# A decoder block on one core: x and the first weights in 256 KB pieces, position loads moved, zero products ahead of the first transposes, x transposed inside the rows

## The chip, the core and the metric

The kernel runs on one core of a Trainium2 chip. The core has a matrix engine (TensorE, PE in the rows), a vector engine (VectorE, DVE), a scalar engine (ScalarE, ACT), GpSimd (POOL) and SyncE (SP), which here only issues transfers. Each engine works through its own list of instructions in order; semaphores make one wait for another. Transfers between the main memory and the on-chip memory run on 16 DMA engines beside them. The metric is the device time of the whole program in microseconds, and less is better.

## What is computed

One decoder block for 256 tokens of width 1024, all in float32: a norm, an input projection, a gated linear attention (GLA) and a softmax attention side by side, an output projection, and a SwiGLU feed-forward part. The change touches only the start, which is the norm and the projection:

```python
def reference(x, positions, norm1_gain, w_in, w_gate_up, b_gate, ...):
    h = rms_norm(x, norm1_gain[l])
    proj = h @ w_in[l]
    gq, gk, gv, gr, g_low, mq, mk, mv = parts      # 256, 256, 512, 512, 16, 512, 512, 512 columns
    gate_logit = (g_low @ w_gate_up[l] + b_gate[l]).astype(jnp.float32)
    log_a = jax.nn.log_sigmoid(gate_logit) / GLA_GATE_TAU
    o_gla = gla_chunked(gq, gk, gv, log_a)          # cumulative sums of log_a
    q_m, k_m = rotary(mq, positions), rotary(mk, positions)
    ...
    x = x + concatenate([o_gla, o_moba]) @ w_out[l]
    x = x + (silu(h2 @ w_ffn_gate[l]) * (h2 @ w_ffn_up[l])) @ w_ffn_down[l]
    return rms_norm(x, final_norm_gain)
```

## The kernel before

**Precision and tiling.** The tokens lie in two tiles of 128 (T = 2), the width in eight chunks of 128 (KC = 8). Every large product is made of three fast ones: an operand is split into a rounded high half and the rest as a low half, and `product` (line 430) issues high x high (L433), high x low weights (L434) and low x high (L435), each with 512 columns. ScalarE makes the high halves, VectorE the low ones.

**Weights.** They come in units of 1 MB (2048 columns of 128 partitions), first into one of three buffers `raw`, then split into one of six `w_hi` and `w_lo`. `split` on ScalarE (L782) and on VectorE (L997) does one unit; semaphores `hi_ready` and `lo_ready` count them. Units 0 and 1 are the eight rows (chunks of 128 input features) of the first 512 columns, that is of gq and gk; two units make one block of 512 columns, six blocks the projection. SyncE issues unit u once the unit three before it has left `raw` (`raw_free`, line 302).

**The start.** SyncE's list: x in two halves of tokens (512 KB each, L278), unit 0 in two halves (L311), the gate's low weights (16 columns of 1024 rows, L313), units 1 and 2, small vectors, and then the gated units. GpSimd issues the positions and rotary frequencies (L369, L370) before it builds the identity matrix (L371, L372), then masks. TensorE transposes the norm's gain (L449), does four transposes of the identity (`warm_up`, L455), then the 16 transposes of x into `aux` (L462), then eight more of the identity. The norm's scale factor per token is applied after the projection, so x can be multiplied at once: ScalarE takes each transposed chunk times the gain into `aT_hi` (`take_xT`, L805), VectorE the low half into `aT_lo` (L1001). Unit 0 is split row by row (`split_first`, L811 on ScalarE, L1013 on VectorE). TensorE's `first_unit` (line 469) waits for all four halves of a row (x and weights, high and low) and then issues its six matmuls.

**After unit 0.** `gate_low` (L495, L496) is a product with the gate's 16 columns, in 16 matmuls of 256 columns. Its weights `low_w` are rounded by ScalarE (L821) and their low half made by GpSimd (L407). VectorE copies the result, `lowT` (L1025), and `logits` (L529) multiply it with the gate's second matrix. VectorE adds the bias (L1034), ScalarE and VectorE make `log_a` (L831 to L833, L1059; the sine's angles, made from the positions, are reduced in between, L1040 to L1065), and `cumulate` (L538, L540), in the middle of unit 3, sums them. The norm's factor `rstd` is made from sums of squares (ScalarE, L788) by two small GpSimd steps for each token tile (L402, L403). These orders are all written out by hand; no scheduler changes them. The rest, attention and eleven feed-forward phases, is not touched but for semaphore counts.

## Time and profile before

| | us |
|---|---|
| median of 3 runs | 314.44 |
| lowest and highest run | 314.31, 314.89 |
| the profiled execution | 314.29 |
| its span in the profile | 312.3 |
| TensorE busy in it | 301.4 |

The rows below come from the one profiled execution. A line of a timeline gives the start and the length of one instruction (or of several alike, with their count behind an x), its engine, its line in the kernel, the operation, what it writes and reads, and in brackets for how long the engine was idle before it and what released it. PE is the matrix engine's products, PEld its loading of the stationary operand, which overlaps them. The ends of matmuls are modelled, so neighbours seem to overlap by 0.1 to 0.2 us: the distance between two starts is what one costs. Counts of matmuls of float32 operands can be multiples of those in the program.

### The profile page before, as it was taken

How to read it: one execution, taken by the hardware profiler on the slowest of the kernel's cores; microseconds unless marked ns; L12 is line 12 of the kernel's file. 1: busy time of each engine (PE TensorE's matmuls, PEld its weight loads, DVE VectorE, ACT ScalarE, POOL GpSimd, SP SyncE). 2: the span in 40 equal slices, each digit the busy share in tenths (PEclk: the TensorE clock that was granted, in tenths of full speed). 3: DMA queues.
4: the chain of work that ended last, by engine and by line, in shares of the span. 5: the costliest groups of instructions: out<-in, count | busy, mean ns of one | idle time of the engine just before them, and what ended most of it. 6: DMA issues, size and time to landing. Idle time of an engine off the chain costs nothing.

```text
span 312.3 us, 3865 instructions
## 1 busy us (share of the span) xinstructions
PE 301.4 (97%) x1424; PEld 251.2 (80%) x1424; DVE 178.9 (57%) x199; ACT 153.7 (49%) x185; POOL 21.9 (7%) x44
## 2 busy tenths in 40 slices
PE   5899999999999999999999999999999999999992
PEld 5787888888888888888888888888888888888881
DVE  0888979986686247645371809082635536280434
ACT  2978897568553437361533526070807152443124
POOL 7130100000202001500000000000000000000002
PEclk9999999999999999999999999999999999999998
DMA  7986386537744303928374564729090918330003
GB/s 224 367 277 244 118 295 206 192 134 270 253 148 139 134 0 82 309 81 283 123 242 163 184 220 137 266 72 331 18 376 9 326 77 274 129 134 0 0 2 135
DMA packets 36449, 54.45 MB, mean 174 GB/s; under 512 B 2834, under 2 KB 25540, under 8 KB 36436
## 3 DMA queue, kind: packets, MB, share of 16 engines
q1 hardware_dynamic: 36356, 54.24, 51.1%
q0 software_dynamic: 64, 0.03, 0.3%
q8 instruction: 8, 0.13, 0.2%
q14 instruction: 5, 0.04, 0.0%
q10 hardware_dynamic: 16, 0.00, 0.0%
HBM read 53.23 MB, written 1.05 MB: 174 GB/s over the span
## 4 chain that ended last, share of the span: by engine, by line
PE 94%; DMA 2%; DVE 1%; ACT 1%; issue 0%; SPq 0%; POOLq 0%; POOL 0%; DVEq 0%
PE acc L433 16%; PE acc L435 15%; PE acc L434 15%; PE aux L435 13%; PE aux L433 13%; PE aux L434 13%; PE aux L522 4%; DMA raw<-in_w_in 2%; PE aux L600 1%; DVE x_sb L1188 1%; PE aux L622 1%; PE aux L582 1%; PE aux L568 1%; DVE reuse_e L1246 0%; ACT reuse_e L974 0%
## 5 line engine op out<-in xcount | busy, mean ns | idle before, releaser
L997 DVE TENSOR_TENSOR w_lo<-raw,w_hi 128x2048 fp32r<-128x2048 f32 x48 | 107.9, 2287 | 15.2 <-ACT w_hi L782 15.2
L782 ACT CAST w_hi<-raw 128x2048 fp32r<-128x2048 f32 x48 | 89.7, 1912 | 6.5 <-PE acc L435 4.6
L433 PE MATMUL aux<-w_hi,aT_hi 128*128 128x512 f32 x176 | 69.7, 396 | 0.0
L435 PE MATMUL aux<-w_hi,aT_lo 128*128 128x512 f32 x176 | 68.8, 391 | 0.0
L434 PE MATMUL aux<-w_lo,aT_hi 128*128 128x512 f32 x176 | 68.5, 389 | 0.0
L433 PE MATMUL acc<-w_hi,aT_hi 128*128 128x512 f32 x136 | 54.9, 403 | 1.1 <-DVE w_lo L1013 1.1
L435 PE MATMUL acc<-w_hi,aT_lo 128*128 128x512 f32 x136 | 53.1, 391 | 0.0
L434 PE MATMUL acc<-w_lo,aT_hi 128*128 128x512 f32 x136 | 53.0, 390 | 0.0
L1220 DVE TENSOR_TENSOR pT_lo<-aux,pT_hi 128x512 fp32r<-128x512 f32 x10 | 6.9, 692 | 70.6 <-ACT pT_hi L943 70.6
L943 ACT CAST pT_hi<-aux 128x512 fp32r<-128x512 f32 x10 | 5.9, 587 | 76.5 <-PE aux L522 76.5
L435 PEld LDWEIGHTS aux<-w_hi,aT_lo 128*128 128x128 f32 x176 | 33.0, 188 | 7.1
L434 PEld LDWEIGHTS aux<-w_lo,aT_hi 128*128 128x128 f32 x176 | 33.1, 188 | 6.6
L433 PEld LDWEIGHTS aux<-w_hi,aT_hi 128*128 128x128 f32 x176 | 33.0, 188 | 6.5
L433 PE MATMUL acc<-w_hi,pT_hi 128*128 128x512 f32 x80 | 31.2, 390 | 0.0
L435 PE MATMUL acc<-w_hi,pT_lo 128*128 128x512 f32 x80 | 31.1, 389 | 0.0
L434 PE MATMUL acc<-w_lo,pT_hi 128*128 128x512 f32 x80 | 31.1, 389 | 0.0
L433 PEld LDWEIGHTS acc<-w_hi,aT_hi 128*128 128x128 f32 x136 | 25.6, 188 | 6.6 <-issue 1.6
L435 PEld LDWEIGHTS acc<-w_hi,aT_lo 128*128 128x128 f32 x136 | 25.5, 188 | 5.5
L434 PEld LDWEIGHTS acc<-w_lo,aT_hi 128*128 128x128 f32 x136 | 25.6, 188 | 4.9
L930 ACT ACTIVATE reuse_c<-aux,rstd 128x256 f32<-128x256 f32 x22 | 10.4, 473 | 26.3 <-PE aux L435 26.2
L434 PEld LDWEIGHTS acc<-w_lo,pT_hi 128*128 128x128 f32 x80 | 15.0, 188 | 3.1
L435 PEld LDWEIGHTS acc<-w_hi,pT_lo 128*128 128x128 f32 x80 | 15.0, 188 | 3.1
(170 smaller groups left out, 237.4 us busy)
## 6 DMA issues: line engine op xcount, KB each, us to landing
raw<-in_w_in SPq DMA_DIRECT2D x24, 512.0 KB, 4.9
raw<-in_w_ffn_gate SPq DMA_DIRECT2D x22, 512.0 KB, 4.4
raw<-in_w_ffn_up SPq DMA_DIRECT2D x22, 512.0 KB, 5.5
raw<-in_w_ffn_down SPq DMA_DIRECT2D x22, 512.0 KB, 5.8
raw<-in_w_out SPq DMA_DIRECT2D x8, 512.0 KB, 4.0
x_sb<-in_x SPq DMA_DIRECT2D x2, 512.0 KB, 3.8
out<-reuse_e SPq DMA_DIRECT2D x4, 256.0 KB, 2.4
reuse_a<-in_final_norm_gain SPq DMA_DIRECT2D x1, 512.0 KB, 4.7
```

What stands on the lines that cost most here:

```text
L433: nc.tensor.matmul(dst, left_hi[:, k, tok], right_hi, start=first, stop=False)
L434: nc.tensor.matmul(dst, left_hi[:, k, tok], right_lo, start=False, stop=False)
L435: return nc.tensor.matmul(dst, left_lo[:, k, tok], right_hi, start=False, stop=last)
L522: last = nc.tensor.transpose(aux[:, bank, n * P:(n + 1) * P], src, ident[:, :])
L568: last = nc.tensor.matmul(aux[:, bank, pair * SEQ:(pair + 1) * SEQ], kiT[:, pair, tok], qdT[:, pair, :, tok], start=True, stop=True)
L582: last = nc.tensor.matmul(aux[:, 2 + h // 2, (h % 2) * SEQ:(h % 2 + 1) * SEQ], mT[:, 0, h, P:SEQ], mT[:, 1, h, :], start=True, stop=True)
L600: last = nc.tensor.matmul(aux[:, bank, h * DV:(h + 1) * DV], probT[:, t + k, h, :], mv[:, k, h * DV:(h + 1) * DV], start=k == 0, stop=k == t)
L782: nc.scalar.copy(w_hi[:, slot % RING, :], raw[:, slot % RAW, :]).then_inc(hi_ready, 1)
L930: nc.scalar.activation(silu_g[:, t, :], aux[:, GATE_UP_BANKS[parity][t], 0:FF], ACT.Silu, scale=rstd[:, 1, t:t + 1]).then_inc(silu_ready, 1)
L943: nc.scalar.copy(dst, aux[:, 1, :].rearrange("p (k s) -> p k s", k=2)).then_inc(hiddenT_hi_ready, 1)
L997: nc.vector.tensor_tensor(w_lo[:, slot % RING, :], raw[:, slot % RAW, :], w_hi[:, slot % RING, :].bitcast(f32), ALU.subtract).then_inc(lo_ ...
L1220: nc.vector.tensor_tensor(lo, aux[:, 1, :].rearrange("p (k s) -> p k s", k=2), hi.bitcast(f32), ALU.subtract).then_inc(hiddenT_lo_ready, 1)
```

## The change

It leaves the computed values' definition as it is and rewrites the first eight rows of weights:

- x comes in four parts of 256 columns for both token tiles, and units 0 and 1 in eight rows of 256 KB, in the order: a part of x, two rows, a part of x, two rows. `EARLY = 2` says that units 0 and 1 are treated by rows; the counts of `hi_ready` and `lo_ready` now begin with unit 2.
- GpSimd issues the positions and the frequencies behind the low half of the gate's weights.
- TensorE begins with six products of a zeroed buffer (`warm`, 256 columns), then the gain's transpose, five more, the first part of x, two more. The zeroing is VectorE's first instruction.
- A row of weights (`first_row`) waits for each of its four halves apart, and rows 1, 3 and 5 hold the four transposes of the next part of x ahead of their last two matmuls.
- `gate_low` and `other_gains` stand behind row 6 and ahead of row 7, `logits` behind row 7.
- VectorE rounds row 0 of the weights itself; the other seven stay with ScalarE, each one ahead of or behind a part of x.

```diff
+EARLY = 2
+X_PARTS = 4
...
-    return u // RAW + (1 if u % RAW else 0)
+    return u // RAW + (1 if u % RAW >= EARLY else 0)
...
+        warm = w_lo[:, RING - 1, 0:SEQ]
...
-            for t in range(T):
-                sp.dma_start(x_sb[:, t, :], x[0, t * P:(t + 1) * P, :]).then_inc(x_loaded[t], 16)
+            def x_part(p):
+                cols = slice(p * 2 * P, (p + 1) * 2 * P)
+                sp.dma_start(x_sb[:, :, cols], x[0, :, cols].rearrange("(t p) n -> p t n", p=P)).then_inc(x_loaded[p], 16)
+
+            def first_part(n):
+                sp.dma_start(raw[:, n // 4, (n % 4) * 512:(n % 4 + 1) * 512],
+                             w_in[0, n * P:(n + 1) * P, BLOCKS[0]:BLOCKS[0] + 512]).then_inc(first_loaded[n], 16)
+
+            for p in range(X_PARTS):
+                x_part(p)
+                for n in (2 * p, 2 * p + 1):
+                    first_part(n)
...
-                if isinstance(u, int) and u == RAW:
-                    sp.wait_ge(first_lo_ready, 4)
+                if isinstance(u, int) and u < RAW + EARLY:
+                    sp.wait_ge(first_lo_ready, 4 * (u - RAW + 1))
                 else:
-                    sp.wait_ge(lo_ready, u - RAW)
-
-            buf = raw[:, 0, :].rearrange("p (k n) -> p k n", k=4)
-            for h in range(2):
-                sp.dma_start(buf[:, 2 * h:2 * h + 2, :], w_in[0, 2 * h * P:2 * (h + 1) * P, BLOCKS[0]:BLOCKS[0] + 512]
-                             .rearrange("(k p) n -> p k n", p=P)).then_inc(first_loaded[h], 16)
+                    sp.wait_ge(lo_ready, u - RAW - EARLY + 1)
+
             sp.dma_start(low_raw[:, :, :], w_in[0, :, LOW:LOW + RANK].rearrange("(k p) n -> p k n", p=P)).then_inc(low_loaded, 16)
-            for u in range(1, RAW):
+            for u in range(EARLY, RAW):
                 rows_unit(u, w_in[0], (u % 2) * 4 * P, 4, BLOCKS[u // 2], 512)
...
-            with nc.allow_non_contiguous_dma(reason="256 positions, one per partition and tile"):
-                pool.dma_start(pos_i[:, :], positions.rearrange("b (t p) -> p (b t)", p=P)).then_inc(pos_loaded, 16)
-            pool.dma_start(freq[:, :], inv_freq.to_broadcast([P, HALF])).then_inc(pos_loaded, 16)
             then(nc.gpsimd.memset(ident[:, :], 0.0))
             nc.gpsimd.affine_select(out=ident[:, :], in_=ident[:, :], compare_op=ALU.not_equal, fill=1.0, base=0,
                                     pattern=[[-1, P]], channel_multiplier=1).then_inc(ident_built, 1)
...
             pool.wait_ge(low_hi_ready, 1)
             nc.gpsimd.tensor_tensor(low_w[:, :, :, 1, :], low_raw[:, :, :].unsqueeze(2).to_broadcast(LOW_COPIES),
                                     low_w[:, :, :, 0, :].bitcast(f32), ALU.subtract).then_inc(low_lo_ready, 1)
+            with nc.allow_non_contiguous_dma(reason="256 positions, one per partition and tile"):
+                pool.dma_start(pos_i[:, :], positions.rearrange("b (t p) -> p (b t)", p=P)).then_inc(pos_loaded, 16)
+            pool.dma_start(freq[:, :], inv_freq.to_broadcast([P, HALF])).then_inc(pos_loaded, 16)
             for t in range(T):
                 wide_rstd(0, t)
...
+            def warm_up(n):
+
+                for _ in range(n):
+                    nc.tensor.matmul(acc[:, 2, 0:SEQ], warm[:, 0:P], warm, start=True, stop=True)
+
+            pe.wait_ge(warm_built, 1)
+            warm_up(6)
             pe.wait_ge(ident_built, 1)
             pe.wait_ge(norm1_loaded, 16)
             nc.tensor.transpose(acc[:, 3, NORM1_ROW:NORM1_ROW + KC], gain_rows[0:KC, :],
                                 ident[0:KC, 0:KC]).then_inc(gains_in_psum, 1)
...
-            def warm_up(n):
-
-                for _ in range(n):
-                    nc.tensor.transpose(acc[:, 2, 0:P], ident[:, :], ident[:, :])
-
-            warm_up(4)
-            for t in range(T):
-                pe.wait_ge(x_loaded[t], 16)
-                for bank in range(4):
-                    for k in (2 * bank, 2 * bank + 1):
-                        last = nc.tensor.transpose(aux[:, bank, (k % 2) * SEQ + t * P:(k % 2) * SEQ + (t + 1) * P],
+            warm_up(5)
+
+            def x_transposed(part):
+
+                pe.wait_ge(x_loaded[part], 16)
+                for k in (2 * part, 2 * part + 1):
+                    for t in range(T):
+                        last = nc.tensor.transpose(aux[:, part, (k % 2) * SEQ + t * P:(k % 2) * SEQ + (t + 1) * P],
                                                    x_sb[:, t, k * P:(k + 1) * P], ident[:, :])
-                    if t == T - 1:
-                        last.then_inc(xT_in_psum, 1)
-
-            warm_up(8)
-
-            def first_unit():
-
-                for k in range(4):
-                    pe.wait_ge(xT_hi_ready, k + 1)
-                    pe.wait_ge(xT_lo_ready, k + 1)
-                    pe.wait_ge(first_hi_ready, k + 1)
-                    pe.wait_ge(first_lo_ready, k + 1)
-                    for t in range(T):
-                        last = product(acc[:, t, :], k, t, *weights(0, 512, k), k == 0, False)
-                last.then_inc(unit_used, 1)
+                last.then_inc(xT_in_psum, 1)
+
+            def first_row(k, next_part=None):
+
+                right_hi, right_lo = weights(k // 4, 512, k % 4)
+                toks = [slice(t * P, (t + 1) * P) for t in range(T)]
+                pe.wait_ge(xT_hi_ready, k + 1)
+                pe.wait_ge(first_hi_ready, k) if k else pe.wait_ge(row0_hi_ready, 1)
+                for t in range(T):
+                    nc.tensor.matmul(acc[:, t, :], aT_hi[:, k, toks[t]], right_hi, start=k == 0, stop=False)
+                pe.wait_ge(first_lo_ready, k + 1)
+                for t in range(T):
+                    nc.tensor.matmul(acc[:, t, :], aT_hi[:, k, toks[t]], right_lo, start=False, stop=False)
+                if next_part is not None:
+                    x_transposed(next_part)
+                pe.wait_ge(xT_lo_ready, k + 1)
+                for t in range(T):
+                    last = nc.tensor.matmul(acc[:, t, :], aT_lo[:, k, toks[t]], right_hi, start=False, stop=k == KC - 1)
+                    if k == KC - 1 and t == 0:
+                        last.then_inc(tile0_in_psum, 1)
+                if k % 4 == 3:
+                    last.then_inc(unit_used, 1)
 
...
-            after = {0: [gate_low, other_gains], 1: [logits], 4: [gla_transposed], 6: [gla_scores],
-                     7: [moba_scores], 9: [moba_outputs]}
-            for u in range(IN_UNITS):
-                if u == 0:
-                    first_unit()
-                else:
-                    in_unit(u, midway.get(u, ()))
+            after = {4: [gla_transposed], 6: [gla_scores], 7: [moba_scores], 9: [moba_outputs]}
+            x_transposed(0)
+            warm_up(2)
+            for k in range(7):
+                first_row(k, next_part=k // 2 + 1 if k in (1, 3, 5) else None)
+            gate_low()
+            other_gains()
+            first_row(7)
+            logits()
+            for u in range(EARLY, IN_UNITS):
+                in_unit(u, midway.get(u, ()))
...
-            def split_first(half):
-                act.wait_ge(first_loaded[half], 16)
-                for k in (2 * half, 2 * half + 1):
-                    nc.scalar.copy(w_hi[:, 0, k * 512:(k + 1) * 512], raw[:, 0, k * 512:(k + 1) * 512]).then_inc(first_hi_ready, 1)
+            def split_first(n):
+                act.wait_ge(first_loaded[n], 16)
+                cols = slice((n % 4) * 512, (n % 4 + 1) * 512)
+                nc.scalar.copy(w_hi[:, n // 4, cols], raw[:, n // 4, cols]).then_inc(first_hi_ready, 1)
 
 
             act.wait_ge(gains_ready, 1)
             take_xT((0, 1))
-            split_first(0)
-            take_xT((2, 3))
-            split_first(1)
-            take_xT((4, 5, 6, 7))
+            for p in range(1, X_PARTS):
+                split_first(2 * p - 1)
+                split_first(2 * p)
+                take_xT((2 * p, 2 * p + 1))
+            split_first(7)
             act.wait_ge(low_loaded, 16)
             nc.scalar.copy(low_w[:, :, :, 0, :], low_raw[:, :, :].unsqueeze(2).to_broadcast(LOW_COPIES)).then_inc(low_hi_ready, 1)
-            split(1)
+            split(2)
             for t in range(T):
-                act.wait_ge(x_loaded[t], 16)
                 sum_squares(0, t)
-            split(2)
             split(3)
             take_block(0, gqk)
...
-            def split_first(k):
-                dve.wait_ge(first_hi_ready, k + 1)
-                cols = slice(k * 512, (k + 1) * 512)
-                nc.vector.tensor_tensor(w_lo[:, 0, cols], raw[:, 0, cols], w_hi[:, 0, cols].bitcast(f32),
+            def split_first(n):
+                slot, cols = n // 4, slice((n % 4) * 512, (n % 4 + 1) * 512)
+                if n:
+                    dve.wait_ge(first_hi_ready, n)
+                else:
+                    dve.wait_ge(first_loaded[0], 16)
+                    nc.vector.tensor_copy(w_hi[:, 0, cols], raw[:, 0, cols]).then_inc(row0_hi_ready, 1)
+                    dve.wait_ge(row0_hi_ready, 1)
+                nc.vector.tensor_tensor(w_lo[:, slot, cols], raw[:, slot, cols], w_hi[:, slot, cols].bitcast(f32),
                                         ALU.subtract).then_inc(first_lo_ready, 1)
 
+            nc.vector.memset(warm.bitcast(f32), 0.0).then_inc(warm_built, 1)
             dve.wait_ge(gains_in_psum, 1)
             nc.vector.tensor_copy(gains[:, 0:KC], acc[:, 3, 0:KC]).then_inc(gains_ready, 1)
             dve.wait_ge(gains_ready, 1)
-            for k in range(4):
-                take_xT((k,))
-                split_first(k)
-            take_xT((4, 5, 6, 7))
-            split(1)
+            split_first(0)
+            take_xT((0, 1))
+            for p in range(1, X_PARTS):
+                split_first(2 * p - 1)
+                split_first(2 * p)
+                take_xT((2 * p, 2 * p + 1))
+            split_first(7)
```

TensorE around the gate's low product, before. `acc` and `aux` are accumulators, `ident` the identity; L433 to L435 are unit 0's last row and unit 1's first, L495 and L496 the low product.

```order
L433 MATMUL acc<-w_hi,aT_hi 128x512
L434 MATMUL acc<-w_lo,aT_hi 128x512
L435 MATMUL acc<-w_hi,aT_lo 128x512
L495 MATMUL acc<-aT_hi,w_hi 128x256 [waits xT_hi_ready,xT_lo_ready,low_lo_ready,low_hi_ready]
L496 MATMUL acc<-aT_lo,w_hi 128x256
...
L483 MATMUL acc<-ident,reuse_d 128x10 [waits rows_loaded,gains_ready]
L433 MATMUL acc<-w_hi,aT_hi 128x512 [waits lo_ready,hi_ready]
L434 MATMUL acc<-w_lo,aT_hi 128x512
L435 MATMUL acc<-w_hi,aT_lo 128x512
```

After, from the transposes inside row 5 on (L488, L491 and L496 are a row's three kinds, L477 the transposes, L517 and L518 the low product):

```order
L477 MATMUL aux<-ident,x_sb 128x128 [waits x_loaded_3]
L477 MATMUL aux<-ident,x_sb 128x128 x3
L496 MATMUL acc<-w_hi,aT_lo 128x512 [waits xT_lo_ready]
...
L488 MATMUL acc<-w_hi,aT_hi 128x512 [waits first_hi_ready,xT_hi_ready]
...
L491 MATMUL acc<-w_lo,aT_hi 128x512 [waits first_lo_ready]
...
L496 MATMUL acc<-w_hi,aT_lo 128x512 [waits xT_lo_ready]
...
L517 MATMUL acc<-aT_hi,w_hi 128x256 [waits xT_hi_ready,xT_lo_ready,low_lo_ready,low_hi_ready]
L518 MATMUL acc<-aT_lo,w_hi 128x256
...
L505 MATMUL acc<-ident,reuse_d 128x10 [waits rows_loaded,gains_ready]
L488 MATMUL acc<-w_hi,aT_hi 128x512 [waits first_hi_ready,xT_hi_ready]
...
L491 MATMUL acc<-w_lo,aT_hi 128x512 [waits first_lo_ready]
```

The low product stood behind four rows and ahead of the other four; it now stands behind seven, and each row's matmuls are grouped by kind with a wait for each.

ScalarE from the second half of unit 0 on, before (L805 takes transposed x, L811 rounds a row, L821 the gate's low weights, L782 a whole unit, L788 the squares):

```order
L811 CAST w_hi<-raw 128x512 [waits first_loaded_1]
L811 CAST w_hi<-raw 128x512
L805 ACTIVATE aT_hi<-aux,gains 128x256 [waits xT_in_psum] x4
L821 CAST w_hi<-low_raw 128x32x16 [waits low_loaded]
L782 CAST w_hi<-raw 128x2048 [waits raw_loaded_1]
L788 ACTIVATE reuse_f,ss<-x_sb 128x1024 [waits x_loaded_0]
L788 ACTIVATE reuse_f,ss<-x_sb 128x1024 [waits x_loaded_1]
L782 CAST w_hi<-raw 128x2048 [waits raw_loaded_2]
```

After, from the rounding of row 6 on (L831, L837, L848, L808 and L814 are the same five):

```order
L837 CAST w_hi<-raw 128x512 [waits first_loaded_6]
L831 ACTIVATE aT_hi<-aux,gains 128x256 [waits xT_in_psum] x2
L837 CAST w_hi<-raw 128x512 [waits first_loaded_7]
L848 CAST w_hi<-low_raw 128x32x16 [waits low_loaded]
L808 CAST w_hi<-raw 128x2048 [waits raw_loaded_2]
L814 ACTIVATE reuse_f,ss<-x_sb 128x1024 x2
L808 CAST w_hi<-raw 128x2048 [waits raw_loaded_0]
```

The low weights' rounding stands behind the last two chunks of x in both, but these now follow the transposes that TensorE does inside row 5.

VectorE, before, from the last chunks of x to the logits' sum (L1001 low half of x, L997 low half of a unit, L1025 the copy of the low product):

```order
L1001 SCALAR_TENSOR_TENSOR aT_lo<-aux,gains,aT_hi 128x256 [waits xT_hi_ready]
L1013 TENSOR_TENSOR w_lo<-raw,w_hi 128x512 [waits first_hi_ready]
L1001 SCALAR_TENSOR_TENSOR aT_lo<-aux,gains,aT_hi 128x256 [waits xT_hi_ready] x4
L997 TENSOR_TENSOR w_lo<-raw,w_hi 128x2048 [waits hi_ready]
L1025 COPY lowT<-acc 32x256 [waits low_in_psum]
L1027 COPY gains<-acc 128x10 [waits gains_in_psum]
L997 TENSOR_TENSOR w_lo<-raw,w_hi 128x2048 [waits hi_ready] x2
```

After (L1043 is the low half of one row, L1022 of a unit, L1058 the copy):

```order
L1043 TENSOR_TENSOR w_lo<-raw,w_hi 128x512 [waits first_hi_ready] x2
L1026 SCALAR_TENSOR_TENSOR aT_lo<-aux,gains,aT_hi 128x256 [waits xT_hi_ready] x2
L1043 TENSOR_TENSOR w_lo<-raw,w_hi 128x512 [waits first_hi_ready]
L1058 COPY lowT<-acc 32x256 [waits low_in_psum]
L1060 COPY gains<-acc 128x10 [waits gains_in_psum]
L1022 TENSOR_TENSOR w_lo<-raw,w_hi 128x2048 [waits hi_ready] x2
```

The split of a whole unit that stood ahead of the copy is gone (it was unit 1's); unit 2's and unit 3's stay behind it.

## Rows read from the trace of the kernel before

**Rows 1.** Page: busy time of each engine; the chain's shares by engine.
```profile
PE 301.4 (97%) x1424; PEld 251.2 (80%) x1424; DVE 178.9 (57%) x199; ACT 153.7 (49%) x185; POOL 21.9 (7%) x44
...
PE 94%; DMA 2%; DVE 1%; ACT 1%; issue 0%; SPq 0%; POOLq 0%; POOL 0%; DVEq 0%
```

**Rows 2.** Chain of waits to 25 us: start, length, what.
```profile
1.71 6.44 DMA raw<-in_w_in
...
9.66 0.47 PE acc L433
```

**Rows 3.** Timeline, TensorE and VectorE: start, length, engine, line, operation.
```profile
15.19 0.28 PE L495 MATMUL acc<-aT_hi,w_hi 128*128 128x256 f32 x1
...
16.98 0.28 PE L496 MATMUL acc<-aT_lo,w_hi 128*128 128x256 f32 x1
...
17.30 0.41 DVE L1025 COPY lowT<-acc 32x256 f32<-32x256 f32 x1
...
24.15 0.50 PE L433 MATMUL acc<-w_hi,aT_hi 128*128 128x512 f32 x1
...
32.45 0.81 PE L538 MATMUL aux<-reuse_b,tri_mid 128*128 128x256 f32 x3
```

**Rows 4.** Tile x_sb, first 25 us: issues on SyncE; from issue to landing.
```profile
L278 SPq DMA_DIRECT2D x_sb<-in_x x2: 382/402/421, 0.8 to 1.2; - x2
...
DMA to landing us min/median/max: 3.4/3.8/4.3
```

**Rows 5.** One window (last: clock, DMA share, GB/s); issues: KB, us to landing.
```profile
6.00:7.00 1.00, 1.00 (x7) 1.00 (x6) 0.00 (x0) 0.00 (x0) 1.00 (x5) 1.00 1.05 218
...
pos_i<-in_positions POOLq DMA_DIRECT2D x1, 1.0 KB, 6.5
```

**Rows 6.** Timeline, TensorE's transposes of the start.
```profile
3.83 1.11 PE L455 MATMUL acc<-ident 128*128 128x128 f32 x4
...
4.74 2.99 PE L462 MATMUL aux<-ident,x_sb 128*128 128x128 f32 x16
...
7.56 1.04 PE L455 MATMUL acc<-ident 128*128 128x128 f32 x8
```

**Rows 7.** Timeline, ScalarE and VectorE on unit 0.
```profile
9.94 1.14 ACT L811 CAST w_hi<-raw 128x512 fp32r<-128x512 f32 x2
...
10.97 1.57 ACT L805 ACTIVATE aT_hi<-aux,gains 128x256 fp32r<-128x256 f32 x4
...
9.83 0.68 DVE L1013 TENSOR_TENSOR w_lo<-raw,w_hi 128x512 fp32r<-128x512 f32 x1
...
10.43 0.48 DVE L1001 SCALAR_TENSOR_TENSOR aT_lo<-aux,gains,aT_hi 128x256 fp32r<-128x256 f32 x1
```

**Rows 8.** Timeline: ScalarE and GpSimd on the low weights, GpSimd beside VectorE.
```profile
12.40 0.65 ACT L821 CAST w_hi<-low_raw 128x512 fp32r<-128x512 f32 x1
...
13.20 1.30 POOL L407 TENSOR_TENSOR w_hi<-low_raw,w_hi 128x512 fp32r<-128x512 f32 x1 [5.39 <-ACT w_hi L821]
...
15.00 2.29 DVE L997 TENSOR_TENSOR w_lo<-raw,w_hi 128x2048 fp32r<-128x2048 f32 x1 [0.93 <-ACT w_hi L782]
...
16.11 1.23 POOL L402 TENSOR_SCALAR ms<-ss 128x1 f32<-128x1 f32 x1 [1.61 <-ACT reuse_f L788]
...
18.08 0.19 POOL L402 TENSOR_SCALAR ms<-ss 128x1 f32<-128x1 f32 x1
...
124.73 2.29 POOL L402 TENSOR_SCALAR ms<-ss 128x1 f32<-128x1 f32 x1 [4.21 <-ACT reuse_f L788]
...
127.10 2.48 POOL L403 TENSOR_TENSOR rstd<-ms,minus_half 128x1 f32<-128x1 f32 x1
```

**Rows 9.** Timeline, VectorE: logits, log gate, low half of unit 4.
```profile
24.26 0.88 DVE L1034 SCALAR_TENSOR_TENSOR reuse_b<-aux,rstd,mv 128x256 f32<-128x256 f32 x2 [0.89 <-PE aux L529]
...
30.08 0.69 DVE L1059 SCALAR_TENSOR_TENSOR reuse_b<-reuse_b 128x512 f32<-128x512 f32 x1
...
32.65 2.28 DVE L997 TENSOR_TENSOR w_lo<-raw,w_hi 128x2048 fp32r<-128x2048 f32 x1
```

14 lines of the change are left out of this document (8 added, 6 removed).

## The prediction

> **What bounds the kernel now.** I read the page first: TensorE is busy for 301.4 us of a span of 312.3 us, VectorE for 57% and ScalarE for 49% of it, and the chain that ended last runs through TensorE for 94% of the span [rows 1]. So the time is set by when TensorE's real work begins and by every gap after that. Then the timeline of the first 35 us, engine by engine. TensorE's first product of the input projection starts at 9.66 us. Before it the chain is one transfer: the first half of unit 0 is issued at 1.71 and lands 6.44 us later; ScalarE rounds it, VectorE subtracts, and TensorE starts [rows 2]. From there TensorE runs nearly without a gap: unit 0's 24 matmuls to 15.19, the gate's low product (16 matmuls of 256 columns) there, then unit 1 and the logits, unit 2 at 24.15, the cumulation at 32.45 [rows 3]. Whatever the change does to the start of unit 2 and of the cumulation is therefore passed on to the end almost one to one. The profiled execution took 314.29 us (2.0 more than its span), 0.15 under the median of the runs, 314.44; all terms below are differences against its trace, added to its 314.29.
>
> **The change part by part.**
>
> *Loads in 256 KB pieces, positions later.* The two transfers of x (512 KB each) are issued at 0.8 and 1.2 and land 3.4 and 4.3 us later, at 4.2 and 5.5 [rows 4]: 1.3 us for 512 KB, so 0.65 for 256 KB once the queue runs. The first piece of x then lands at 4.2 - 0.65 = 3.55, the first row of weights at 4.2, and each further piece 0.65 later: x parts at about 3.6, 5.5, 7.5, 9.4, the last row of weights at 10.7, the gate's low weights about a microsecond behind. Between 6 and 7 us the traffic was 218 GB/s, against the 400 of 512 KB in 1.3 us; the positions, which GpSimd's queue brings, landed about then, 6.5 us after their issue [rows 5], so I take the moved issue to remove this dip. An upper bound is that the dip stays: pieces behind the fifth then come up to 1.3 us later, which still hides, because a pair of rows needs three pieces (1.95 us) and takes longer than that (below). GpSimd's two issues no longer stand ahead of the identity, so the gain transpose can run before 3.83 [rows 6]; I take the identity as there when the first six products end, at 2.65. If it were there only at 3.6, the whole start would come 0.5 to 0.9 us later.
>
> *Zero products.* No row of before has them; the gate's 256-column matmuls follow each other at 0.12 us (16.98 back to 15.19 over 15) [rows 3], and the start runs at half the clock: four transposes of the identity took from 3.83 to 4.74, 0.23 apart, eight later ones 1.04 in all, 0.11 apart [rows 6]. That is 1.2 and 2.4 GHz, although the granted clock reads 1.00 in the window of rows 5. So 0.24 us per zero product at the low clock. VectorE's memset, begun with the first issues at 0.8, ends at about 1.1 (a 128x256 VectorE step took 0.48 [rows 7], the upper end), six products run to 2.65, the gain transpose to 2.85, five products to 4.05. TensorE is then free 0.5 us after the x piece landed, so the filling work costs up to 0.5 us of that transfer's gain. Four transposes give the first part at 4.75 (clock up) to 5.1 (clock low); I take 4.9. The sixteen transposes of x took 2.99 us [rows 6]: with 0.27 for the last, 15 gaps fill 2.72, which makes about ten of 0.21 and five of 0.11, so the clock rose at about 6.9, 3.1 us after the row at 3.83, with nothing but transposes run. With the first product now at 1.2, the rise comes from 4.4 on; the upper bound is where it came before, 6.9.
>
> *Rows.* ScalarE takes a part of x in 0.47 us, 0.36 apart in a run [rows 7]. Hand-overs took 0.04 (16.98 + 0.28 to VectorE's 17.30 [rows 3]) to 0.15 (ScalarE's 12.40 + 0.65 to GpSimd's 13.20 [rows 8]); I take 0.10 into ScalarE and 0.11 into TensorE. Row 0 starts at 4.9 + 0.10 + 0.47 + 0.11 = **5.6** instead of 9.66. The rounding that VectorE now makes for row 0 is bounded by 0.34 and 0.68 (half of and all of its 128x512 subtraction [rows 7]); from 4.2 either is done before 5.6. A matmul of 512 columns costs 0.2275 us (24 from 9.66 to 15.19, the first 0.31 [rows 2, 3]), a row of six 1.365. In before, the 16 transposes ran while TensorE waited for weights anyway; now 12 of them lie inside rows 1, 3 and 5, and the next part depends on them. The loop from one part's transposes to the next is: 0.10 + 0.47 + 0.11 (ScalarE's step and the hand-overs, TensorE idle), five pairs of matmuls 5 x 0.455 = 2.275, four transposes 4 x 0.11 + 0.16 until the last one's end, and about 0.09 in waits for the low half of the odd row's weights: **3.65 us per two rows**. TensorE's own work in it is 2.73 + 0.44 = 3.17; ScalarE's is 2 x 0.57 + 2 x 0.36 = 1.9 at most (the rounding at half of 1.14) and VectorE's 2 x 0.68 + 2 x 0.48 = 2.3 at most [rows 7], so neither binds, and the supply (1.95) doesn't. The last part is transposed at 4.9 + 3 x 3.65 = **15.85**.
>
> *The gate's low product.* ScalarE rounds its weights only after that part: 0.10, two takes of 0.37, the last row's rounding 0.52 (0.57 at most), the low weights 0.65: 17.86. GpSimd follows 0.15 later with 1.30 us [rows 8]. VectorE is then subtracting row 7 (17.65 to 18.3), and here the trace shows a lock. GpSimd's one-column multiply (line 402) takes 0.19 us when VectorE is idle, but took 1.23 when it came at 16.11 into VectorE's subtraction of 15.00 to 17.29, and 2.29, the length of such a subtraction, at 124.73 [rows 8]. So GpSimd starts at 18.3 and ends at 19.65, and TensorE, which has finished row 6 at 17.9, waits 1.8 us and begins the product at **19.8** instead of 15.19. The Trainium skill (SBUF — State Buffer, Who interferes with whom) says that a VectorE instruction with two SBUF inputs and a GpSimd one that reads SBUF exclude each other, the first to issue keeping the port; these rows agree. Were GpSimd not held, the sum would be 0.3 lower.
>
> *Unit 2.* The product needs 2.07 us to its last result (15.19 to 17.26), and VectorE, in order, copies it before it splits unit 2: copies 0.48 (0.41 of it [rows 3] plus one of ten columns), subtraction 2.29, hand-overs 0.18, together 2.95 [rows 3, 8]. Unit 1's split stood ahead of this copy before, and unit 2's right behind it. Now TensorE is through row 7 and the logits at 24.4 and unit 2 starts at 19.8 + 2.07 + 2.95 = **24.8**, against 24.15: +0.65.
>
> *Cumulation.* VectorE's subtraction for unit 3 ends at 26.9, and the logits step follows it, where it started at 24.26 before (it waited for TensorE then). The log gate ended at 30.77, 6.5 later [rows 9]; so at 33.4 now. TensorE comes to the cumulation at 24.8 + 8.30 = 33.1 and waits until 33.5: +0.4. Unit 4's low half shifts by 2.6 from 34.94 (32.65 + 2.29 [rows 9]). TensorE came to unit 4 at 36.9 (32.45, some 1.75 of cumulation, twelve matmuls of 0.2275), comes 1.05 later now, and so finds it done by a hair: nothing more waits. GpSimd's position issues now stand behind the low weights, to about 21.2, ahead of the norm's factor, whose input comes at 20.8 to 21.9; by the 6.5 us of before they land at 26 to 27 and are wanted at 27.7.
>
> *Rows at the low clock.* If the clock rises before 5.6 they cost nothing, if at 6.9 half of 1.34 us less what is hidden by a wait of 0.17: 0.5. I take 0.2.
>
> Sum: -4.06 for row 0's start, then the in-row transposes, hand-overs, gate wait and split give +0.65 at unit 2, +0.4 at the cumulation, +0.2 for the clock: **+1.25**. 314.29 + 1.25 = 315.54 by the profiled execution, 315.69 by the median; I say 315.6.
>
> **The rivals.**
>
> *The rows run at TensorE's pace (faster).* If ScalarE's step is covered (its hand-overs shorter than I add, TensorE's queued instructions starting without the gap), the loop is 3.17 to 3.25 instead of 3.65. Three loops give back 1.2 to 1.4, and the gate, unit 2 and the cumulation move with them. With the clock term gone too the sum is 1.25 - 1.4 - 0.2 = -0.35, and with GpSimd not held -0.65: 313.7 to 314.1. It turns faster than before below 3.23 us per loop. For it speaks that the whole idea gives TensorE a head start of 4 us; against it, that the in-order wait for the next part is in the program and that each hand-over in the rows costs at least 0.04.
>
> *GpSimd held twice.* Its multiply for token tile 1 comes at 22.15, VectorE's subtraction of unit 2 at 22.4. If the order flips, it is held like at 124.73, and its power step behind it like at 127.10 (2.48) [rows 8], so the factor comes at 27.4 instead of 25.2. The logits step then waits 0.5: 316.1. A late landing of the positions costs VectorE, and with it the cumulation, about as much.
>
> *The clock stays low.* If the waits between the first rows keep it at 1.2 GHz to 8 or 9 us, rows 0 and 1 and the transposes cost another 0.8 to 1.3 over my term: 316.5 to 317.
>
> *Small pieces are dear.* The first transfer took 3.4 us, 1.3 of it for its bytes by the distance to the second [rows 4], so 2.1 are fixed. Were that paid by every piece in turn, one came every 2.75 us, the last row's at 3.55 + 11 x 2.75 = 34 us instead of 10.7, and row 7 would end some 13 us later than now: 328. Two queued transfers landed 1.3 us apart, which speaks against it; I give it 1 in 100. The Trainium skill (DMA: Bandwidth & Descriptors, Anatomy of one DMA) also names about 2.0 us fixed for a transfer, and its section on bandwidth advises pieces of 1 MiB and more.
>
> **How the numbers follow.** My forecast (315.1 to 316.0) has 0.45, the faster rival 0.13, a half-way loop (3.3 to 3.5, 314.1 to 315.0) 0.2, GpSimd held twice 0.12, the low clock 0.09, dear pieces 0.01. The likeliest gives 315.6. The range reaches from 314.1, leaving out most of the faster rival, to 316.9, within the low clock's. A measurement of this kernel can tell about 0.2%, 0.63 us, from no change: under 313.8 is faster, over 315.07 slower. Faster takes 0.11, since part of its rival ends above 313.8; same 0.23; slower 0.66.
>
> **What would show it.** Right: row 0's first product at 5.4 to 5.9; gaps of 0.3 to 0.5 us ahead of rows 2, 4 and 6, released by ScalarE's take; a wait of 1.3 to 2 us ahead of the low product, released by GpSimd; one of about half a microsecond ahead of unit 2, released by VectorE; unit 2 at 24.5 to 25.1. Wrong: a low product that starts before 18.8, or no gap ahead of it; rows that follow each other without ScalarE as releaser; a first piece of x that lands after 4.2; matmuls spaced 0.43 beyond row 1.

## The result and the profile after

The changed kernel took 316.44 us (median of 20 runs, 316.01 to 319.1), against 314.97 (20 runs, 314.31 to 317.61) for the kernel before in the same comparison: a ratio of 1.0038, 95% interval 1.0020 to 1.0057. It is slower, by about what was forecast: 1.47 by the medians, against 1.25 in the sum. Six of the 20 runs of the kernel before took 317.1 to 317.6, and the ratio is below that of the medians (1.0047). The profiled execution took 316.05 us with a span of 314.1, against 314.29 and 312.3.

The page of the changed kernel (busy time, then the chain by engine), beside [rows 1]:

```profile
PE 303.8 (97%) x1425; PEld 250.7 (80%) x1425; DVE 180.0 (57%) x204; ACT 153.6 (49%) x187; POOL 25.9 (8%) x44
...
PE 90%; DVE 3%; POOL 3%; ACT 2%; issue 1%; POOLq 0%; DVEq 0%; ACTq 0%
```

No transfer stands in the chain any more, but GpSimd, VectorE and ScalarE do, with 8% together where they had 2%. TensorE's own timeline shows where (start, length, engine, line, operation, in brackets the idle time ahead and its releaser; PEld is the loading of row 2's stationary operand):

```profile
5.94 0.73 PE L488 MATMUL acc<-w_hi,aT_hi 128*128 128x512 f32 x2 [0.36 <-ACT aT_hi L831]
...
9.54 0.30 PEld L488 LDWEIGHTS acc<-w_hi,aT_hi 128*128 128x128 f32 x2 [0.53 <-ACT aT_hi L831]
9.54 0.73 PE L488 MATMUL acc<-w_hi,aT_hi 128*128 128x512 f32 x2
...
15.59 0.60 PE L477 MATMUL aux<-ident,x_sb 128*128 128x128 f32 x4
...
16.76 0.73 PE L488 MATMUL acc<-w_hi,aT_hi 128*128 128x512 f32 x2
...
19.80 0.36 PE L517 MATMUL acc<-aT_hi,w_hi 128*128 128x256 f32 x1 [1.39 <-POOL w_hi L415]
...
24.76 0.47 PE L444 MATMUL acc<-w_hi,aT_hi 128*128 128x512 f32 x1
...
33.93 0.48 PE L560 MATMUL aux<-reuse_b,tri_mid 128*128 128x256 f32 x1 [0.74 <-DVE reuse_b L1092]
```

| milestone (us) | before | forecast | after |
|---|---|---|---|
| row 0's first product | 9.66 | 5.6 | 5.94 |
| two rows and a part's transposes | - | 3.65 | 3.60 |
| last part of x transposed | - | 15.85 | 16.2 |
| low product starts | 15.19 | 19.8 | 19.80 |
| unit 2 starts | 24.15 | 24.8 | 24.76 |
| cumulation starts | 32.45 | 33.5 | 33.93 |
| profiled execution | 314.29 | 315.54 | 316.05 |

So TensorE is 3.7 us ahead at row 0. The low product starts 4.6 later than before, with seven rows ahead of it where there were four. At unit 2, with the same work done in both, the change is 0.6 behind, at the cumulation 1.5 and at the end 1.8. Matched one by one, the later matmuls lose 0.1 within the cumulation, 0.1 at the transposes of the keys (59.8 in the trace before) and less than 0.1 after that.

The other engines, in the same columns, ahead of the low product and of the logits step:

```profile
16.23 0.84 ACT L831 ACTIVATE aT_hi<-aux,gains 128x256 fp32r<-128x256 f32 x2 [1.74 <-PE aux L477]
...
17.47 0.63 ACT L848 CAST w_hi<-low_raw 128x512 fp32r<-128x512 f32 x1
...
18.25 1.45 POOL L415 TENSOR_TENSOR w_hi<-low_raw,w_hi 128x512 fp32r<-128x512 f32 x1 [11.82 <-ACT w_hi L848]
...
22.17 0.19 POOL L410 TENSOR_SCALAR ms<-ss 128x1 f32<-128x1 f32 x1
22.44 4.84 POOL L411 TENSOR_TENSOR rstd<-ms,minus_half 128x1 f32<-128x1 f32 x1
...
22.39 4.47 DVE L1022 TENSOR_TENSOR w_lo<-raw,w_hi 128x2048 fp32r<-128x2048 f32 x2
27.37 0.88 DVE L1067 SCALAR_TENSOR_TENSOR reuse_b<-aux,rstd,mv 128x256 f32<-128x256 f32 x2 [0.51 <-issue]
```

ScalarE takes the last part of x at 16.23, and the low weights stand two steps behind it: that is the chain to 19.80. Then GpSimd's power step for tile 1 begins 0.05 us behind VectorE's subtraction for unit 2 and is held through it and the one for unit 3: it ends at 27.28, and only 0.09 later the logits step begins. The timeline puts the idle 0.51 ahead of it down to issue, but the step reads that factor. Every later VectorE step up to the log gate (33.19) is late by it.

### The profile page after: what moved, and what is told of

It reads as the page before. It is cut to its first block, busy times and chain, and to the rows that moved or that the text cites. A ratio compares the mean times of both kernels' runs of the same rounds, so it can differ in the third digit from the quotient of the medians.

```text
span 314.1 us, 3879 instructions
## 1 busy us (share of the span) xinstructions
PE 303.8 (97%) x1425; PEld 250.7 (80%) x1425; DVE 180.0 (57%) x204; ACT 153.6 (49%) x187; POOL 25.9 (8%) x44
## 3 DMA queue, kind: packets, MB, share of 16 engines
HBM read 53.23 MB, written 1.05 MB: 173 GB/s over the span
## 4 chain that ended last, share of the span: by engine, by line
PE 90%; DVE 3%; POOL 3%; ACT 2%; issue 1%; POOLq 0%; DVEq 0%; ACTq 0%
PE acc L446 13%; PE acc L444 13%; PE acc L445 13%; PE aux L446 13%; PE aux L444 13%; PE aux L445 13%; PE aux L544 4%; POOL rstd L411 2%; PE acc L488 1%; DVE reuse_e L1083 1%; PE acc L461 1%; PE acc L491 1%; PE aux L622 1%; ACT aT_hi L831 1%; PE aux L477 1%
## 5 line engine op out<-in xcount | busy, mean ns | idle before, releaser
L1022 DVE TENSOR_TENSOR w_lo<-raw,w_hi 128x2048 fp32r<-128x2048 f32 x47 | 105.5, 2286 | 12.4 <-ACT w_hi L808 12.3
L808 ACT CAST w_hi<-raw 128x2048 fp32r<-128x2048 f32 x47 | 87.8, 1911 | 7.7 <-PE acc L446 4.6
L444 PE MATMUL acc<-w_hi,aT_hi 128*128 128x512 f32 x120 | 48.4, 404 | 0.0
L446 PE MATMUL acc<-w_hi,aT_lo 128*128 128x512 f32 x120 | 46.9, 391 | 0.0
L445 PE MATMUL acc<-w_lo,aT_hi 128*128 128x512 f32 x120 | 46.8, 390 | 0.0
L446 PEld LDWEIGHTS acc<-w_hi,aT_lo 128*128 128x128 f32 x120 | 22.5, 188 | 4.9
L444 PEld LDWEIGHTS acc<-w_hi,aT_hi 128*128 128x128 f32 x120 | 22.6, 188 | 4.7 <-issue 0.4
L445 PEld LDWEIGHTS acc<-w_lo,aT_hi 128*128 128x128 f32 x120 | 22.6, 188 | 4.4
```

The costliest lines, as they stand in the source:

```text
L444: nc.tensor.matmul(dst, left_hi[:, k, tok], right_hi, start=first, stop=False)
L445: nc.tensor.matmul(dst, left_hi[:, k, tok], right_lo, start=False, stop=False)
L446: return nc.tensor.matmul(dst, left_lo[:, k, tok], right_hi, start=False, stop=last)
L808: nc.scalar.copy(w_hi[:, slot % RING, :], raw[:, slot % RAW, :]).then_inc(hi_ready, 1)
L1022: nc.vector.tensor_tensor(w_lo[:, slot % RING, :], raw[:, slot % RAW, :], w_hi[:, slot % RING, :].bitcast(f32), ALU.subtract).then_inc(lo_ ...
```

## The experiments

Each is the changed kernel with the edit shown, unless it says otherwise. "Span" is that of the profiled execution, and times in the text are from its trace; the change itself has 316.44, 1.0038 and 314.1. The kernel before had medians of 314.75 to 314.97 in these comparisons, so medians can differ by 0.2 with nothing changed, and by the ratios the gains over the change are 0.1 to 0.6 us smaller than by the medians. The fastest run of the change took 316.01; 9 of the 12 runs with the low weights early, 9 of 12 with unit 2's subtraction first and 11 of 12 with the factors free took less.

| kernel | median us | ratio to before, 95% | span |
|---|---|---|---|
| low product behind row 7 | 316.67 | 1.0055, 1.0039 to 1.0072 | 314.7 |
| low weights rounded early | 315.77 | 1.0025, 1.0005 to 1.0044 | 314.6 |
| transposes first in the row | 314.92 | 1.0005, 0.9987 to 1.0024 | 314.0 |
| unit 2's subtraction first | 315.30 | 1.0020, 1.0000 to 1.0041 | 313.5 |
| factors free | 315.80 | 1.0020, 1.0001 to 1.0039 | 313.4 |
| no zero products | 317.75 | 1.0085, 1.0057 to 1.0113 | 315.3 |
| positions first again | 318.22 | 1.0094, 1.0064 to 1.0124 | 315.2 |
| four zero products before row 0 | 316.63 | 1.0052, 1.0035 to 1.0069 | 314.9 |
| pieces of 512 KB | 320.00 | 1.0156, 1.0138 to 1.0174 | 317.8 |
| rows and low weights | 314.26 | 0.9982, 0.9966 to 0.9998 | 312.0 |
| short chain | 313.90 | 0.9961, 0.9945 to 0.9977 | 312.4 |
| short chain, unit 4 sooner | 313.10 | 0.9944, 0.9922 to 0.9966 | 311.3 |

### Is the wait ahead of the low product lost time?

```diff
-            gate_low()
-            other_gains()
             first_row(7)
+            gate_low()
+            other_gains()
             logits()
```

> The changed kernel, with the gate's low product moved behind row 7 of the first block on TensorE; nothing else. Theory: the 1.4 us wait ahead of the low product is not lost TensorE time but the tail of a chain (last part of x, ScalarE's roundings, GpSimd's low half, low product, VectorE's copy, its subtraction for unit 2). Row 7 then runs in the wait, the low product still starts at 19.8 us and unit 2 at 24.7 to 24.9 (24.76 with the change): 316.4 us, within 0.3. Rival: what counts is the sum of TensorE's idle time, so that filling 1.4 us of it brings the end forward as much: unit 2 at 23.4, 315.0 us.

Measured: 316.67 us. Row 7 ran in the wait, the low product started at 19.94 all the same and unit 2 at 24.92. The rival is out: filling TensorE's idle time brings nothing, since unit 2 comes 0.1 behind the end of VectorE's subtraction and TensorE waits 1.19 for it. The trace shows one cost that neither theory had. TensorE's idle time now lies behind the low product (0.35 and 1.19 us), and the record of the granted clock falls from full to half at 25.57 and comes back at 28.98. In between, matmuls are 0.43 us apart instead of 0.23:

```profile
24.92 0.47 PE L444 MATMUL acc<-w_hi,aT_hi 128*128 128x512 f32 x1 [1.19 <-issue]
...
27.05 0.63 PE L444 MATMUL acc<-w_hi,aT_hi 128*128 128x512 f32 x1
27.47 0.63 PE L445 MATMUL acc<-w_lo,aT_hi 128*128 128x512 f32 x1
...
34.79 0.59 PE L560 MATMUL aux<-reuse_b,tri_mid 128*128 128x256 f32 x2
```

The cumulation starts 0.9 us later than with the change and no longer waits. Other executions probably have this fall too: the mean granted clock is 0.990 to 0.993 in 10 of the 12 runs, where no run of the change is under 0.994. The fastest, with 0.998, took 316.07, which is no better than the change's fastest.

### The low weights earlier on ScalarE

```diff
                 split_first(2 * p)
+                if p == X_PARTS - 1:
+                    act.wait_ge(low_loaded, 16)
+                    nc.scalar.copy(low_w[:, :, :, 0, :], ...).then_inc(low_hi_ready, 1)
                 take_xT((2 * p, 2 * p + 1))
             split_first(7)
-            act.wait_ge(low_loaded, 16)
-            nc.scalar.copy(low_w[:, :, :, 0, :], ...).then_inc(low_hi_ready, 1)
```

> The changed kernel, with ScalarE rounding the gate's low weights ahead of its take of the last part of x instead of behind the last row; nothing else. Theory: GpSimd's low half is ready by 17.4 us, the low product starts right behind row 6 at 18.3 to 18.5 instead of 19.80, unit 2 at 23.3 to 23.5, the logits step at 25.6 to 26.1; the wait before the cumulation stays between 0.4 and 0.9. 314.7 to 315.2 us. Rival: the factor that GpSimd makes late alone sets the cumulation, and unit 2's earlier start is spent waiting there: 316.2 to 316.4.

Measured: 315.77 us, lowest run 314.87; the theory's size was reached in the best runs only. The profiled execution is one of the slower ones and shows why they differ: the clock rose at 9.59 us, not at 5.23. Up to row 2 its program is the change's, yet row 2 starts at 11.19 instead of 9.54, because rows 0 and 1 ran at half the clock (two matmuls in 1.05 us, 0.43 apart, instead of 0.62):

```profile
7.82 1.05 PE L496 MATMUL acc<-w_hi,aT_lo 128*128 128x512 f32 x2
8.67 1.05 PE L488 MATMUL acc<-w_hi,aT_hi 128*128 128x512 f32 x2
...
16.81 1.55 POOL L415 TENSOR_TENSOR w_hi<-low_raw,w_hi 128x512 fp32r<-128x512 f32 x1 [10.78 <-ACT w_hi L847]
...
19.92 0.28 PE L517 MATMUL acc<-aT_hi,w_hi 128*128 128x256 f32 x1
...
22.45 2.71 POOL L411 TENSOR_TENSOR rstd<-ms,minus_half 128x1 f32<-128x1 f32 x1
25.24 2.04 POOL L410 TENSOR_SCALAR ms<-ss 128x1 f32<-128x1 f32 x1
```

GpSimd's low half was ready at 18.36, and the low product followed row 6 without a wait, at 19.92. So the wait is gone, and at unit 2 (24.82) what was saved had gone to the late clock in this execution. A second loss, which the theory didn't have, follows: GpSimd's power step for tile 0 (2.71) and its multiply for tile 1 (2.04) are held by one subtraction each, so the factor for tile 1 comes at 27.91 instead of 27.28, and the cumulation waits 1.32. The edit alone is worth 0.7 us by the medians, 0.4 by the ratios.

### Where the rows' pace comes from

```diff
+                if next_part is not None:
+                    x_transposed(next_part)
                 pe.wait_ge(xT_hi_ready, k + 1)
 ...
-                if next_part is not None:
-                    x_transposed(next_part)
                 pe.wait_ge(xT_lo_ready, k + 1)
```

> The changed kernel, with the transposes of the next part of x at the start of rows 1, 3 and 5 instead of behind their fourth matmul; nothing else. Theory: the 3.6 us per two rows is the serial loop through ScalarE's take (its 0.48 and two hand-overs with TensorE idle). With a whole row between the transposes and the row that needs them it is hidden, the loop takes TensorE's own 3.17 to 3.25, the low product starts at about 17.9 and unit 2 at about 22.9: 314.4 to 314.8 us. Rival: the rows are paced by the supply (rows of weights landed 0.7 to 2.1 apart) or by ScalarE and VectorE, the loop stays at 3.5 or more: 316.0 to 316.4.

Measured: 314.92 us, 1.5 less than the change, though the profiled execution again had a late clock (9.39). From row 2 on it shows the pace undisturbed:

```profile
10.98 0.63 PE L490 MATMUL acc<-w_hi,aT_hi 128*128 128x512 f32 x2
...
14.19 0.62 PE L490 MATMUL acc<-w_hi,aT_hi 128*128 128x512 f32 x2
...
17.39 0.62 PE L490 MATMUL acc<-w_hi,aT_hi 128*128 128x512 f32 x2
...
19.78 0.36 PE L517 MATMUL acc<-aT_hi,w_hi 128*128 128x256 f32 x1 [0.85 <-issue]
```

Rows 2, 4 and 6 start 3.20 us apart instead of 3.61, with the same supply. That is TensorE's own work (3.17 in the prediction), so the supply, ScalarE and VectorE don't pace the rows; the place of the transposes in the row does. The gain itself shows in the medians only: in this execution the late clock used it up, the low product starts at 19.78 and the cumulation at 33.92, as with the change.

### VectorE's order and GpSimd's factor

```diff
             split_first(7)
+            split(2)
             dve.wait_ge(low_in_psum, 1)
 ...
-            split(2)
             split(3)
```

> The changed kernel, with VectorE's subtraction for unit 2 ahead of its copies of the low product and of the gains instead of behind them; nothing else. Theory: VectorE was idle for 3.4 us ahead of these copies, so the subtraction runs there from 20.0; unit 2 starts when TensorE has made row 7 and the logits, at about 24.5 (0.26 earlier), the subtraction for unit 3 ends at 25.2 instead of 26.9, the logits step starts by 25.8 and the cumulation waits for nothing: 1.0 less, 315.4 us. Rival: only unit 2's start counts, 316.1; or GpSimd, held by the subtractions one after the other, still brings the factor at 27 or later: 316.1 to 316.4.

Measured: 315.30 us, as the theory said (315.4). The subtraction for unit 2 ran in VectorE's idle time, and GpSimd was held only by one subtraction (1.04 us at 21.84); TensorE waits nowhere behind the low product, and the cumulation starts at 33.61, although this execution's clock rose at 6.96, its low product came at 20.4 and unit 2 at 25.28. So the gain comes at the logits step (26.62 instead of 27.37) and not at unit 2.

```profile
20.53 2.29 DVE L1022 TENSOR_TENSOR w_lo<-raw,w_hi 128x2048 fp32r<-128x2048 f32 x1 [1.35 <-ACT w_hi L808]
...
26.62 0.87 DVE L1067 SCALAR_TENSOR_TENSOR reuse_b<-aux,rstd,mv 128x256 f32<-128x256 f32 x2
...
33.61 0.59 PE L560 MATMUL aux<-reuse_b,tri_mid 128*128 128x256 f32 x2
```

The second edit leaves VectorE alone and frees GpSimd (the factors ahead of the positions' issues, the sums ahead of unit 2's rounding):

```diff
+            for t in range(T):
+                wide_rstd(0, t)
             pool.dma_start(pos_i[:, :], ...)
             pool.dma_start(freq[:, :], ...)
-            for t in range(T):
-                wide_rstd(0, t)
 ...
-            split(2)
             for t in range(T):
                 sum_squares(0, t)
+            split(2)
             split(3)
```

> The changed kernel, with ScalarE's two sums of squares ahead of its rounding of unit 2, and GpSimd's issues of the positions behind its two factors; nothing else. Theory: GpSimd then makes both factors between 19.7 and 21.5 us, while VectorE waits for the low product, and isn't held for 4.84 us by the subtractions of units 2 and 3. The logits step starts at 26.9 instead of 27.36, the wait of 0.74 ahead of the cumulation falls to 0.25: 315.9 to 316.1 us by the median of 316.44 with the change. Rival: the factor isn't what the logits step waits for, it starts at 27.3 all the same: 316.4.

Measured: 315.80 us, a little better than expected. The power step takes 0.55 us, and the logits step follows the subtraction at once:

```profile
20.99 0.55 POOL L411 TENSOR_TENSOR rstd<-ms,minus_half 128x1 f32<-128x1 f32 x1
...
26.81 0.86 DVE L1067 SCALAR_TENSOR_TENSOR reuse_b<-aux,rstd,mv 128x256 f32<-128x256 f32 x2
...
33.36 0.92 PE L560 MATMUL aux<-reuse_b,tri_mid 128*128 128x256 f32 x3 [0.17 <-DVE reuse_b L1092]
```

The cumulation starts 0.57 earlier than with the change, with unit 2 in the same place (24.78): that is what the hold cost.

### The start, part by part

Without the zero products:

```diff
-            warm_up(6)
 ...
-            warm_up(5)
 ...
-            warm_up(2)
```

> The changed kernel without its 13 zero products, so that TensorE does nothing before the transposes but the one of the gains; nothing else. Theory: the transposes start a little earlier, at 4.0 to 4.2 us, but the clock rises later, after 7 us, and rows 0 and 1 (and part of 2) run with 0.43 us per matmul instead of 0.23; each part of x is transposed later by that, the low product starts 1 to 2 us later: 317.3 to 318.2 us. Rival: the rise comes when it would have come anyway, or is hidden behind the waits of the rows: 316.1 to 316.5.

Measured: 317.75 us. The clock rose at 9.05; row 0 started 0.4 us earlier than with the change, row 2 at 10.71, 1.2 later, the low product at 20.96.

```profile
5.52 1.22 PE L486 MATMUL acc<-w_hi,aT_hi 128*128 128x512 f32 x2 [0.63 <-ACT aT_hi L828]
...
10.71 0.73 PE L486 MATMUL acc<-w_hi,aT_hi 128*128 128x512 f32 x2
```

With the positions issued first again:

```diff
+            pool.dma_start(pos_i[:, :], ...)
+            pool.dma_start(freq[:, :], ...)
             then(nc.gpsimd.memset(ident[:, :], 0.0))
 ...
-            pool.dma_start(pos_i[:, :], ...)
-            pool.dma_start(freq[:, :], ...)
             for t in range(T):
                 wide_rstd(0, t)
```

> The changed kernel, with GpSimd issuing the positions and the frequencies first of all, as before the change; nothing else. Theory: the identity is there 1 us later, so the gain transpose comes at 3.8 us instead of 2.82, the five zero products behind it and with them the first part's transposes 0.9 us later, and all rows too: low product at 20.6, 317.2 us. The dip that their packets make in the traffic costs nothing, since the first rows aren't bound by the supply. Rival: the dip is what counts, rows of weights land a microsecond later and the rows wait for them, 317.6 or more; or neither, 316.4.

Measured: 318.22 us. The profiled execution does what the theory says (317.13 us in all): gain transpose at 3.63, row 0 at 6.76, low product 1.1 us late. The median is 1.1 above it, which the theory doesn't give; row 0's weights also landed later (VectorE starts on them at 5.76 instead of 4.45) and the clock rose at 7.48. I could not tell these two apart. The six runs lie at 317.1 (two), 317.9 and 318.5 to 318.6 (three).

```profile
3.63 0.27 PE L467 MATMUL acc<-ident,reuse_d 8*128 8x8 f32 x1 [0.73 <-POOL ident L383]
...
6.76 1.06 PE L488 MATMUL acc<-w_hi,aT_hi 128*128 128x512 f32 x2 [0.20 <-ACT aT_hi L831]
```

With the gap before row 0 filled:

```diff
             x_transposed(0)
-            warm_up(2)
+            warm_up(4)
```

> The changed kernel with four zero products instead of two between the transposes of the first part and row 0; nothing else. They fill the 0.5 us in which TensorE stood idle before row 0. Theory: what differs between executions of the changed kernel and of those like it is when the clock rises (5.2 us in one profile, 7.0 and 9.4 to 9.6 in others, the rows before it at 0.43 us per matmul); with the gap filled it rises before row 1 in all of them, and the median comes to the lowest runs of the change, 316.0 to 316.1 instead of 316.44. Rival: the gap has no part in that, median 316.4 to 316.7, with row 0 up to 0.2 us later.

Measured: 316.63 us; the theory is out. From 2.83 to row 0 the timeline names no idle time of TensorE any more, and the clock still rose only at 7.63, during row 0:

```profile
5.12 1.20 PE L461 MATMUL acc<-w_lo 128*128 128x256 f32 x4
6.12 1.20 PE L488 MATMUL acc<-w_hi,aT_hi 128*128 128x512 f32 x2
7.11 0.88 PE L491 MATMUL acc<-w_lo,aT_hi 128*128 128x512 f32 x2
7.83 0.63 PE L496 MATMUL acc<-w_hi,aT_lo 128*128 128x512 f32 x2
```

With x and the rows in 512 KB transfers:

```diff
-            for p in range(X_PARTS):
-                x_part(p)
-                for n in (2 * p, 2 * p + 1):
-                    first_part(n)
+            for half in range(2):
+                cols = slice(half * 4 * P, (half + 1) * 4 * P)
+                sp.dma_start(x_sb[:, :, cols], ...).then_inc(x_loaded[2 * half], 16)
+                for n in (4 * half, 4 * half + 2):
+                    sp.dma_start(raw[...], w_in[0, n * P:(n + 2) * P, ...]).then_inc(first_loaded[n], 16)
```

> The changed kernel with x and the rows of weights in six transfers of 512 KB (half of x, rows 0 and 1, rows 2 and 3, and again) instead of twelve of 256 KB; everything else is the change's. Theory: the first half of x lands at 4.2 us, when TensorE is still busy with zero products, rows 0 and 1 at about 5.5, so VectorE rounds row 0 at 5.5 instead of 4.8 and TensorE starts it at 6.1 instead of 5.94; the later ones come in time. The rows' pace (3.6 us per two) is that of the loop through ScalarE, not of the supply: low product at 20.0, unit 2 at 24.9, 316.4 to 316.8 us. Rival: the pieces of 256 KB are what makes the early start, row 0 comes at 6.5 or later and the rows wait for their weights: 317.2 or more. Or the small pieces were dear (their rows of weights landed 0.7 to 2.1 us apart) and the larger ones bring a gain: 316.0 or less.

Measured: 320.00 us, 3.6 more than the change: the first rival. The half of x landed at about 5.2 and rows 0 and 1 at 7.1, not at 4.2 and 5.5:

```profile
5.30 1.12 PE L472 MATMUL aux<-ident,x_sb 128*128 128x128 f32 x4 [0.83 <-DMA x_sb<-in_x]
...
7.17 0.43 DVE L1036 CAST w_hi<-raw 128x512 fp32r<-128x512 f32 x1 [3.86 <-DMA raw<-in_w_in]
...
12.09 0.60 PE L472 MATMUL aux<-ident,x_sb 128*128 128x128 f32 x4
```

TensorE waited 0.83 and 0.90 us, the clock rose at 11.99 only, rows 0 and 1 ran at half of it, and the second part was transposed at 12.09 instead of 8.38. So 1.8 us are lost by row 0 (7.74) and as much again by row 2 (13.25). My theory had taken the landing at 4.2 from [rows 4], where a transfer was one token tile of x with both tiles first in the queue; why the same 512 KB landed a microsecond later here is open. Small pieces are not dear here; with what the late clock adds they are worth over 3 us.

### A version that beats both

The transposes first and the low weights early, together (the two diffs above):

> The changed kernel with two of the short chain's four moves: the transposes at the start of rows 1, 3 and 5, and ScalarE's rounding of the low weights ahead of its take of the last part of x. VectorE's order is the change's. Theory: these two carry the gain; low product at about 17.3 us, unit 2 at 22.2 to 22.4, the cumulation at 30.9 to 31.3: 313.7 to 314.1 us, no more than 0.2 behind the short chain. Rival: GpSimd's factor for tile 1, held by both subtractions, and the copy behind which VectorE's subtraction for unit 2 stands take back half of it: 314.5 or more.

Measured: 314.26 us, between the two. The low product starts at 17.5 and unit 2 at 22.4 as expected, but GpSimd's multiply for tile 1 is held 4.27 us, and the cumulation waits 1.0:

```profile
20.32 4.27 POOL L410 TENSOR_SCALAR ms<-ss 128x1 f32<-128x1 f32 x1 [0.18 <-ACT reuse_f L814]
...
31.87 1.13 PE L560 MATMUL aux<-reuse_b,tri_mid 128*128 128x256 f32 x4 [1.01 <-DVE reuse_b L1093]
```

With VectorE's order changed too: the subtraction for unit 2 first, as above, and the log gate step among the steps on the angles:

```diff
-            for part in two_pi_parts(5):
+            for n, part in enumerate(two_pi_parts(5)):
                 take_off(turns_hi.bitcast(f32), part)
+                if n == 2:
+                    dve.wait_ge(soft_ready, 1)
+                    nc.vector.scalar_tensor_tensor(out=log_a, ...).then_inc(log_a_ready, 1)
                 take_off(turns_lo, part)
-            dve.wait_ge(soft_ready, 1)
-            nc.vector.scalar_tensor_tensor(out=log_a, ...).then_inc(log_a_ready, 1)
```

> The changed kernel with four moves: transposes of the next part at the start of rows 1, 3 and 5; ScalarE's rounding of the low weights ahead of its take of the last part of x; VectorE's subtraction for unit 2 ahead of its copies of the low product; VectorE's log gate step between its steps on the angles, after 5 of the 10, where it stood behind all 10. Theory: the change loses time only in the chain from the last part of x to unit 2 and in the log gate's chain, and both can be shortened. Row 6 ends at about 17.0 us, the low product starts there (19.8 with the change), unit 2 at 21.5 to 22.1 (24.76; 24.15 before the change), the cumulation at 29.8 to 30.6 (33.91; 32.46 before the change): 312.3 to 313.2 us. Rival: the time comes back further on, since the loads and roundings of units 4 to 9 can't keep up with a TensorE that is 3 us ahead, or VectorE's order makes units 3 or 4 late: 314.0 us or more.

Measured: 313.90 us, short of the theory. The low product starts at 17.7, unit 2 at 22.5 and the cumulation at 30.87, each 0.3 to 0.7 later than in the theory (this execution's clock rose at 7.14), but the last 1.6 ahead of [rows 3]. Then 1.1 us went at unit 4 and 0.4 at the transposes of the keys: VectorE came to unit 4's subtraction only at 34.10, one of the angle steps ahead of it having taken 1.08 beside a fill of GpSimd's:

```profile
32.82 0.96 POOL L423 MEMSET reuse_b<- 128x1024 f32 x1 [10.29 <-PE aux L562]
...
32.78 1.08 DVE L1099 TENSOR_SCALAR reuse_e<-reuse_e 128x128 f32<-128x128 f32 x1
...
34.10 4.49 DVE L1023 TENSOR_TENSOR w_lo<-raw,w_hi 128x2048 fp32r<-128x2048 f32 x2
```

The short chain with unit 4 served sooner, on ScalarE and on VectorE:

```diff
             nc.scalar.activation(soft, soft, ACT.Ln, ...)
-            nc.scalar.preload_act_table(ACT.Exp)
             split(4)
+            nc.scalar.preload_act_table(ACT.Exp)
 ...
+            split(4)
             nearest_turns()
             for part in two_pi_parts(3):
                 take_off(turns, part)
 ...
-            split(4)
             split(5)
```

> The kernel of the short chain, with unit 4 served sooner: ScalarE rounds it ahead of loading the table for Exp instead of behind it, and VectorE subtracts it ahead of the second half of the steps on the angles. In the short chain the cumulation came 1.65 us earlier than before the change, but unit 4 only 0.5 us earlier, since its subtraction started at 34.10 behind all the angle steps (one of them 0.85 us long for a fill of GpSimd's). Theory: that subtraction now starts at 31.3 to 31.5, unit 4 isn't waited for, and the 1.1 us are kept to the end: 312.6 to 313.1 us. Rival: the angles, the operands of the gate's attention or unit 5 come late in its place and take it back at 40 to 60 us: 313.6 to 314.0.

Measured: 313.10 us, 0.9944 of the kernel before, faster than both kernels. The subtraction starts at 31.20, unit 4 waits for nothing, and one wait of 0.55 is left at the keys' transposes:

```profile
31.20 2.29 DVE L1023 TENSOR_TENSOR w_lo<-raw,w_hi 128x2048 fp32r<-128x2048 f32 x1
...
58.62 1.09 PE L544 MATMUL aux<-ident,reuse_e 128*128 128x128 f32 x8 [0.55 <-DVE reuse_e L1116]
```

## Why the prediction was right, and where its steps were off

The chain that was foreseen is the one in the trace: early rows with ScalarE's step in their loop, a low product that waits for ScalarE's and GpSimd's roundings of its weights, VectorE's subtraction for unit 2 behind that, and a small loss at the cumulation. The edits that shorten this chain each gained, and the one that only filled the wait gained nothing. One step was wrong, that GpSimd's factor is ready in time. The time itself lies in the stated range but above the band of 315.1 to 316.0 that had the best chance; 0.5 of the 0.84 above 315.6 is the kernel before, which took 314.97 in this comparison instead of 314.44.

- *The signs.* Row 0 came just past the 5.4 to 5.9 named. The loading ahead of rows 2, 4 and 6 sat idle for 0.53 each time, released by ScalarE's take, and their first products come 0.49 behind the last of the row ahead, where the spacing is 0.23. The wait ahead of the low product was 1.39, but that ahead of unit 2 was 0.1 and not half a microsecond: VectorE's subtraction ended at 24.66, and by the spacing without a wait (0.30 behind the last logits matmul) TensorE would have come there at 24.67 itself. None of the signs of being wrong came.
- *Row 0* came at 5.94, not 5.6. The zero products ended at 4.26 instead of 4.05, the four transposes ran at the low clock (the upper value of the step, 5.1, and then 0.2 more), so ScalarE took the part at 5.42.
- *Supply.* I put the dip in traffic down to the positions. They are gone from the start, and the dip is still there, only earlier (windows of one microsecond of the changed kernel; the last number is GB/s), beside [rows 5]:

```profile
4.00:5.00 1.00, 1.00 (x8) 1.00 (x6) 0.52 (x2) 0.00 (x0) 1.00 (x4) 1.00 0.76 220
5.00:6.00 1.00, 0.64 (x5) 0.43 (x3) 0.69 (x1) 0.58 (x2) 0.94 (x4) 1.00 0.95 257
```

  Its cause is open. Pieces came later than the 0.65 apart that I took: ScalarE waited 0.71 for row 2's weights. It hid, as the step's upper bound said.
- *Rows* took 3.60 instead of 3.65 us per two; with row 0 that puts the last part at 16.2 instead of 15.85.
- *Low product* at 19.80: exact by luck, since two errors cancelled. ScalarE ended its rounding at 18.10 instead of 17.86, and GpSimd started 0.15 behind it while VectorE was subtracting row 7 and took 1.45 in all, instead of waiting for the subtraction's end and then taking 1.30. The wait was 1.39 and not 1.8, because row 6 also ended later (18.41 instead of 17.9, of which some 0.15 is its modelled end).
- *Cumulation.* This term was mis-sized: a wait of 0.74 instead of 0.4, and a start at 33.93 instead of 33.5. The step took GpSimd's factor as ready; I had made its being held a rival with 0.12 and priced it with one subtraction per instruction, which gave 27.4 for the factor; it came at 27.28, by one step held through two. So part of what brought the result is that rival's. It happened in all seven traces with the change's order of these steps (4.84 to 4.96 us), through both subtractions, and freeing the factor brought the cumulation 0.57 forward.
- *Clock.* 0.2 was a mean that no execution shows. In the profiled one the clock rose at 5.23, ahead of row 0, and the term is nothing. In others with the same start it is large: row 2 was 1.65 us late with a rise at 9.59. The step's upper bound for the rise, 6.9, didn't hold. The median stands 0.39 above the profiled execution, and the spans of the change's runs lie, but for two, at 314.1 to 314.3 (8 runs) or at 314.4 to 314.9 (10 runs); that the clock's rise makes this difference is my reading. The mean granted clock of each run divides these 18 in the same way, 0.997 or 0.998 for the eight and 0.994 or 0.995 for the ten, but it covers the end of the run too and doesn't say when the clock rose.
- After the cumulation's start another 0.28 was lost, for which the sum had nothing.

Together: 1.05 foreseen at the cumulation, 0.43 more there and 0.28 behind it make the 1.76 of the profiled execution. The faster rival was a real one: its pace of 3.17 to 3.25 needs only the transposes moved to the row's start, and then the kernel is level with the one before. The rival of small dear pieces points the wrong way by over 3 us.

## What to carry to other kernels

An earlier start is worth only what the next join lets through: list everything that the first in-order wait behind it needs from every engine, and move those steps up too. The head start of 3.7 us brought nothing over the kernel before until the transposes and ScalarE's rounding of the gate's low weights had been moved up by a few lines. An idle engine is not a loss by itself: fill the wait and nothing is gained; shorten the chain that it waits for.

## What the runs showed of the hardware

- A GpSimd instruction on one column is held not by one VectorE subtraction but by as many as follow each other at once: 4.84 us at 22.44 with the change and 4.27 at 20.32 in the version with rows and low weights, against 0.55 (the power step) and 0.19 (the multiply) when free and 2.29 and 2.48 in [rows 8]. With the low weights early the second subtraction started only 0.22 behind the first, and the power step got in between them after 2.71. The Trainium skill (SBUF — State Buffer, Who interferes with whom) has the exclusion itself, and these rows agree. A GpSimd fill, which only writes, took 0.96 us beside VectorE's subtractions, and these kept their length (35.99 beside the two from 35.76 in the change). But in the short chain the same fill began 0.04 behind a VectorE step with one input, and that step took 1.08 instead of 0.23 (34.91 in the version with unit 4 sooner). That the fill held it is inferred from this one trace.
- TensorE's clock rose at 5.23 with the change, at 7.63 with even less idle time ahead, and at 9.39 and 9.59 in two kernels whose start is almost the same. Idle time ahead of it isn't the whole cause. Ahead of this first rise every trace reads a granted clock of 1.00 although the spacings are those of the low clock (zero products 0.21 apart): the record begins with the rise, and before it only the spacing tells the clock. The Trainium skill (TensorE: Matmul & The Clock Gate, Part 1: The HAM clock gate) says that the number of matmuls at the low clock differs from run to run of one kernel. No two traces here are of the same kernel, but the change (5.23) and the version with the low weights early (9.59) have the same program up to row 5, which agrees; what decides it stays open here. It also fell back in the middle of a kernel, at 25.57, after two idle times of 0.35 and 1.19 us close together; one of 1.39 in the change was followed by no fall.
- Splitting the first transfers in two brought VectorE's first step on the weights from 7.17 to 4.45 us, with 512 KB instead of 1 MB to move until then.
